# The one-window way of the expert stage is written before the two-window way, behind the same branch

## The reference

```python
group_probs = softmax(t @ w_rg + b_rg)
p_group, g_idx = top_k(group_probs, 1)                # one of 4 groups for each token
in_group = (logits of the 8 experts of that group)
p_exp, e_idx = top_k(softmax(in_group), 2)            # two experts of the group
...
for gi in range(4):                                   # 8 experts of each group
    act = silu(t @ w_g[e]) * (t @ w_u[e])
    out += (act * combine[:, e]) @ w_d[e]
x = x + g2 * out
```

## Time and profile before

| | |
|---|---|
| median of 3 runs | 2145.35 us (2141.6 to 2146.05) |
| the profiled execution | 2147.72 us |
| its span | 2145.4 us |
| mean granted TensorE clock | 0.974 of full speed |
| PE busy | 2027.1 us, 94% |
| DVE busy | 1644.5 us, 77% |
| ACT busy | 1085.7 us, 51% |
| expert stage, layer 0 | branch near 248 us, last scatter ends near 560 us |
| expert stage, layer 1 | branch near 748 us, last scatter ends near 1061 us |

### The profile page before, as it was taken

The page is one execution under the profiler, slowest core; times in us unless marked ns, Lnnn a source line. Parts: engine busy times, 40 slices in busy tenths (PEclk is TensorE's granted clock), DMA queues, the critical chain, the costliest instruction groups (busy, mean ns, idle before and its releaser), DMA issues.

```text
span 2145.4 us, 30818 instructions
## 1 busy us (share of the span) xinstructions
PE 2027.1 (94%) x11923; PEld 1794.3 (84%) x11923; DVE 1644.5 (77%) x2190; ACT 1085.7 (51%) x1564; POOL 70.2 (3%) x111
## 2 busy tenths in 40 slices
PE   4969899999899899999899999999999999999998
PEld 4858788888788878888799989889989998888998
DVE  6968698999799689999778875766657887676555
ACT  2002487787402277877743455554455345555444
POOL 0200000000020000000000001100000000020000
PEclk7989799999999899999999999999999999999999
DMA  8969688987676859888949985167673998515651
GB/s 314 238 236 346 275 312 336 377 335 296 233 273 245 335 204 377 334 336 337 330 156 333 330 240 138 59 237 275 236 248 132 335 349 257 134 64 177 216 177 40
DMA packets 266932, 547.03 MB, mean 255 GB/s; under 512 B 31026, under 2 KB 187180, under 8 KB 242220
## 3 DMA queue, kind: packets, MB, share of 16 engines
q1 hardware_dynamic: 266796, 545.17, 71.9%
HBM read 540.94 MB, written 4.19 MB: 254 GB/s over the span
## 4 chain that ended last, share of the span: by engine, by line
PE 68%; DVE 18%; ACT 4%; issue 4%; SPq 2%; DMA 2%; POOL 1%; DVEq 0%; ACTq 0%; POOLq 0%; PEldq 0%
PE ps L759 9%; DVE acc L1897 6%; PE ps L701 6%; PE ps L732 6%; PE ps L734 5%; PE ps L733 5%; PE ps L807 5%; PE ps L809 5%; PE ps L808 5%; DVE arena L2015 3%; PE ps L847 2%; PE ps L849 2%; PE ps L848 2%; DVE wsp L1936 2%; SPq L457 2%
## 5 line engine op out<-in xcount | busy, mean ns | idle before, releaser
L2174 DVE TENSOR_TENSOR ring_lo<-ring,wsg 128x1024 fp32r<-128x1024 f32 x384 | 459.4, 1223 | 45.8 <-ACT wsg L1496 38.9
L1936 DVE TENSOR_TENSOR wsp<-ring,wsp 128x1024 fp32r<-128x1024 f32 x264 | 321.8, 1224 | 185.6 <-ACT wsp L1448 178.4
L1448 ACT ACTIVATE wsp<-ring 128x1024 fp32r<-128x1024 f32 x264 | 278.1, 1057 | 334.8 <-PE ps L734 245.3
L1496 ACT ACTIVATE wsg<-ring 128x1024 fp32r<-128x1024 f32 x384 | 405.4, 1059 | 82.4 <-PE ps L809 55.1
L732 PE MATMUL ps<-hsp,wsp 128*128 128x256 f32 x1408 | 401.1, 285 | 5.3 <-DVE hsp L2352 3.1
L733 PE MATMUL ps<-hsp,wsp 128*128 128x256 f32 x1408 | 398.4, 283 | 0.0
L734 PE MATMUL ps<-hsp,wsp 128*128 128x256 f32 x1408 | 398.3, 283 | 0.0
L701 PE MATMUL ps<-arena,ring 128*128 128x256 f32 x1280 | 286.0, 384 | 22.0 <-DMA ring<-in_w_in_dram 18.6
L701 PEld LDWEIGHTS ps<-arena,ring 128*128 128x128 f32 x1280 | 244.9, 192 | 57.9 <-DMA ring<-in_w_in_dram 19.1
L732 PEld LDWEIGHTS ps<-hsp,wsp 128*128 128x128 f32 x1408 | 270.0, 192 | 8.3 <-DVE wsp L1936 3.9
L733 PEld LDWEIGHTS ps<-hsp,wsp 128*128 128x128 f32 x1408 | 270.2, 192 | 0.7
(11 more groups left out here) (265 smaller groups left out, 2663.4 us busy)
## 6 DMA issues: line engine op xcount, KB each, us to landing
ring<-in_w_expert_gate_dram SPq DMA_DIRECT2D x64, 1024.0 KB, 6.9
ring<-in_w_expert_up_dram SPq DMA_DIRECT2D x64, 1024.0 KB, 9.1
ring<-in_w_expert_down_dram SPq DMA_DIRECT2D x64, 1024.0 KB, 5.1
ring<-in_ada_w_dram SPq DMA_DIRECT2D x48, 1152.0 KB, 8.8
ring<-in_ffn_w_gate_dram SPq DMA_DIRECT2D x44, 1024.0 KB, 11.8
ring<-in_ffn_w_up_dram SPq DMA_DIRECT2D x44, 1024.0 KB, 13.9
ring<-in_ffn_w_down_dram SPq DMA_DIRECT2D x44, 1024.0 KB, 5.2
ring<-in_w_ada_dram SPq DMA_DIRECT2D x32, 1152.0 KB, 12.9
```

What stands on the lines that cost most here:

```text
L1496: act_(high_piece(n % HIGHS, j), piece(EXPERT_1[e], j), ACT.Identity).then_inc(S.whi, 1)
L1936: v_.tensor_tensor(split_part(at % SPLITS, 1, n), piece(unit, n), split_part(at % SPLITS, 0, n, F32), ALU.subtract).then_inc(S.wlo, 1)
L2174: v_.tensor_tensor(low_piece(EXPERT_1[e], j), piece(EXPERT_1[e], j), high_piece(n % HIGHS, j, F32), ALU.subtract).then_inc(S.wlo, 1)
```

## The change

The condition of the branch is turned round on the three engines, and the bodies of its two sides change places. The one-window way now stands first behind the branch, where the stream goes on without a jump, and the two-window way second. Before, it was the other way round. Neither body is changed within. An engine that has run the first body jumps over the second; one that has run the second simply goes on.

```diff
@@ PE
-                with pe.If(fullest > P):
+                with pe.If(fullest <= P):
+                    gather(1)
+                    experts(l, 1)
+                with pe.Else():
                     gather(2)
                     experts(l, 2)
-                with pe.Else():
-                    gather(1)
-                    experts(l, 1)
@@ ACT
-                with eng.If(fullest > P):
-                    second_exp()
-                    gather(2)
-                    experts(l, 2)
-                with eng.Else():
+                with eng.If(fullest <= P):
                     experts(l, 1, early=True)
                     second_exp()
                     gather(1)
                     experts(l, 1)
+                with eng.Else():
+                    second_exp()
+                    gather(2)
+                    experts(l, 2)
@@ DVE
                 before_moe = own.n
-                with eng.If(fullest > P):
-                    experts(2)
+                with eng.If(fullest <= P):
+                    experts(1)
                 after_moe = own.n
                 own.use(dve_experts)
                 own.n = before_moe
                 with eng.Else():
-                    experts(1)
+                    experts(2)
```

## The result

| | us, median (lowest to highest) | ratio to before, 95% interval |
|---|---|---|
| before | 2145.35 (2141.6 to 2146.05) | 1 |
| after | 2160.02 (2154.48 to 2162.0) | 1.0062 (1.0048 to 1.0076) |

Both medians are of five executions. The change makes the kernel 0.62% slower, by 10 to 16 us. The forecast was slower too, but by 5.8 us: 2151.2 us, in a range up to 2157.5 us. The measured time lies above that range.

What follows compares the result with a forecast made beforehand. The prediction took PE, busy 94% of the span, as the bound. Entry gains of 0.17 and 0.63 us and exit losses of 3.3 us twice gave +5.8 us on 2145.35: 2151.2 us, range 2145.0 to 2157.5.

Steps and rivals of the forecast that it cites:

- 5.9 was taken: PE's exit jump over the two-window way, priced at 5.9 us by the old entry's branch rows.
- (c): Exit: PE's jump takes less than 2.6 us and is hidden, leaving the entry's 0.8 us gain; 2144.6 us, chance 0.13.
- (e): Branch layout: the first body isn't laid out behind the branch, and nothing changes; 2145.35 us, chance 0.04.
- (f): Entry: the fall-through has to fetch as well, so the entry stays as it was; +6.6, 2152.0 us, chance 0.05.
- (d): Entry: PE bound the gather after all, giving -8.8 us against the exits' +6.6; 2143.2 us, chance 0.03.
- when the exit's jump begins: Stage end on PE: jump begins 1.9 us behind line 863's wait, making lines 711 and 1106 3.3 us late each.
- (b): Exit costs more: jump begins with the last product (2156.0 us), or the clock falls in new idle stretches; chance 0.15.
- rows 10 and 11: Profile rows at a PE loop's end, read as the sequencer ahead of its array, sending instructions at 0.06 us each.
- The clock, taken as 0: Clock loss after PE's idle stretch at the entry, counted as 0, with 1.7 us a layer kept for the range.
- -0.17 and -0.63: Entry gains in us for layers 0 and 1, small because ACT, held in `second_exp()`, limits PE's earlier gather.
- Should one of them fetch, PE's longer jump covers most of it: ACT's and DVE's exits: expected jumps of 45 to 67 ns, with any fetch mostly hidden under PE's jump.
- The rule weighed: Fetch rule: alone, it moves one fetch per layer from entry to exit, sum zero; rows gave the places unlike cover.

Runs made afterwards that it cites:

- free banks: Changed kernel, the last scatter's four parts given PSUM banks 6, 7, 3, 2, so the third and fourth don't wait for DVE: 2153.15 us, ratio 1.0026.
- work under the jump: Changed kernel plus 18 extra fp32 products of 128 columns on PE behind the last scatter, ahead of the exit's jump: 2163.93 us, ratio 1.0086.
- long work under the jump: Changed kernel plus 6 extra fp32 products of 512 columns on PE behind the last scatter, ahead of the exit's jump: 2159.09 us, ratio 1.0064.
- At the entry work under the jump: Kernel before plus 3 extra fp32 products of 512 columns on PE between the count's loading and the entry's branch: 2149.22 us, ratio 1.0021.
- PE's order put back: Changed kernel with the exchange undone on PE and kept on ACT and DVE: 2149.4 us, ratio 1.0015.
- no far code: Changed kernel with PE's never-taken two-window way (its Else and two calls) taken out: 2150.58 us, ratio 1.0025.
- PE's hint alone: Changed kernel with a branch hint for PE's exit jump, placed at the head of the one-window body, none on DVE: 2150.2 us, ratio 1.0024.
- first control: Kernel before plus 4 extra fp32 products of 128 columns behind the last scatter in each layer: 2149.51 us, ratio 1.0017.

## Why the prediction was right in its sign and wrong in its size

**What held.** PE's branch is a fetch of code, and the change moves it from the entry to the exit in each layer (0.09 us there, 6.05 and 6.40 us here; 5.9 was taken). PE starts line 1054 right behind line 2140, ACT in `second_exp()` holds the gather, and PE stands idle between the second and third step of line 1074, as written. The delay of lines 711 and 1106 passes through to ACT's lines 1422 and 1621 in full. Rivals (c), (e) and (f) fall with the branches' rows, and (d) with ACT's hold on the gather.

**The step that failed: when the exit's jump begins.** I let it begin 1.9 us behind line 863, by the 32 instructions behind that wait at 0.06 us each, because "the later waits travel with the products". They do, but the branch waits for their release. In after it began at 555.8, with the release of the fourth part's wait for DVE, 2.95 us behind the first product; with the waits taken away (free banks) it began 0.1 us behind the first product, with almost all the products still ahead. So the 0.06 us were no price at all, and 3.3 us an exit became 5.14 and 5.50. In the terms of the sum: the jump begins 2.95 and 2.97 us behind the first product, where 1.2 and 1.3 were taken, and lasts 6.05 and 6.40 us in place of 5.9. Rival (b), with 0.15, had the right direction and not the mechanism: it let the jump begin with the last product, 3.7 us behind the first, which is 5.7 us an exit and 11.4 for both. Its 10.6 us are that less the 0.8 us of the entry, so it is chance that they look like the 10.64 us of the two exits. Free banks speak against its rule: there the jump does not follow the array.

**Why rows 10 and 11 misled.** They do show the sequencer ahead of the array, and I took the 1.6 us from line 716's wait to the loop's branch for the time of sending 24 instructions. Two other causes fit. Line 716's wait itself was not passed early: it stands at 1173.2, and line 759's load ahead of it was released at 1173.16:

```profile
1173.16 0.99 PEld L759 LDWEIGHTS ps<-wsp,asp 128*128 128x128 f32 x5 [0.52 <-DVE wsp L1936]
```

And when the branch began, at 1174.8, line 718's 12 loads and 4 of line 759 were still to run, with as many matmuls, some 32 to 34 instructions: the full queue of the run with work under the jump. By this reading the sequencer was not sending at a pace, it waited for a place. (Two small slips do not change this: 1.6 us by 24 instructions is 0.067 us and not 0.06, and the chances that make up "slower" add up to 0.735 and not 0.72.)

**The clock, taken as 0.** The prediction named the loss in line 711 and put it with rival (b), and named 1.7 us a layer for the entry as a bound. It came to 2.26 us at line 711 and 0.45 behind line 1106. The entry, worth -0.17 and -0.63, came to +0.87 and +0.34: ACT's part was right in kind, but PE's fourth and fifth steps ran at the lower clock, and ACT then waited for PE. Of the 8.8 us between the forecast's 5.8 and the balance's 14.6, 4.0 are the exits, 2.7 the clock behind them and 2.0 the entries; so the exits' start is the largest miss and not the only one, and the entries' part is no larger than the scatter of single executions. I had the row for it and let the value be 0 where it stood for a loss. The run with long work under the jump shows the link between the idle time and line 711's clock. At the entry work under the jump lifted the clock of line 1054, and it fell again with the 1.74 us of idle time that followed.

**DVE.** "Should one of them fetch, PE's longer jump covers most of it" fits what happened. In the three runs in which DVE has the new order and PE's exit costs little (PE's order put back, no far code, PE's hint alone), a stall of 5.4 to 5.5 us shows at layer 1's exit, and 2.6 us of it are exposed (line 1122's wait of 5.19 us in place of 2.56). That it is a fetch is inferred, from its size, from the missing releaser and from the hint that took it away. In the changed kernel no row shows it.

**The rule weighed.** The Trainium skill (Runtime: NRT & Kernel Launch, section Instruction fetch mechanics) has a taken branch to code that isn't held wait for a fetch. The runs agree: 6.05 to 6.40 us without a hint, 0.31 to 0.35 us with one. The 51 ns for a branch that is always taken, in the Trainium skill (Advanced Engine Details and Errata, section Control Flow Timing), are near ACT's and DVE's branches (38 and 53 to 61 ns, which the trace records as compare-and-branch), and far from PE's exits.

**What stays open.** The interval of the ratio leaves 10.3 to 16.3 us for a balance of 14.6, so the small terms (the entry, the clock) are read from single executions and not shown by the times. Why the first control's 16 instructions gave a second stall at layer 1 and none at layer 0, and why DVE stalls at layer 1's exit and not at layer 0's, may depend on where the code lies in memory, which no run measured.

## What to carry to other kernels

A jump over thousands of instructions cost PE a fetch here, some 6 us, at the entry and at the exit alike; place it where the engine waits for others anyway, as the kernel before does, or hint it from the head of the body. Count its start from the release of the last wait ahead of it, not from the last product, and look behind the branch too: idle time of "issue" a few instructions on may be such a fetch. When one engine's stall is taken away, look for the one on another engine that lay under it; here ACT's and DVE's new order showed 3.3 us by itself and nothing on top of PE's.

## What the runs showed of the hardware that I had not expected

- A far branch on PE began as soon as the last wait ahead of it was released (555.7 us in free banks), with 15 of 16 recorded matmuls and their loads not yet begun. With more work queued, it began with some 34 to 36 instructions still ahead (559.1 us in work under the jump).
- The hint at the head of the body, with some 1,340 recorded matmuls and as many loads between it and the jump, still served the jump at its end: 6.05 and 6.40 us became 0.35 and 0.31.
- A stall with no releaser can stand some instructions behind the branch: 5.45 us on DVE and 3.41 us on PE, with the branch itself at 0.3 us or less, and 4.43, 2.76 and 1.57 us on PE behind a branch that had taken some 6 us.
- With 16 more instructions a layer, ahead of a branch that they don't touch, a stall of 1.57 us appeared behind its target in layer 1.
- Behind 4.98 us of idle time (after) PE ran at 1.2 GHz for 4.5 us, and line 711 took 5.88 us; behind 2.71 us (free banks) line 711 took 5.41 us; with no idle time ahead of it, 3.62 us.
